# Output projections finished tile by tile over three slabs, and the first token tile turned inside the last slab

## The reference

```python
x = layer_norm(ALPHA * x + h, g, b)        # layers 0 and 1, three times each
x = x + gate * h;  n = rmsnorm(x)          # later layers (adaptive norm)
# h is always  (something of 256 x K) @ w_out, K = 1024, 2048 or 2816
# the next stage is always  norm(x) @ w_in
```

## Time and profile before

| | |
|---|---|
| time, median of 3 runs | 2055.17 us (2053.49 to 2056.4) |
| the profiled execution: its own time | 2055.43 us |
| the profiled execution: its span | 2053.7 us, so 1.73 us lie around it |
| PE busy | 1920.8 us, 94% of the span |
| POOL, DVE, ACT busy | 61%, 54%, 49% |
| mean granted TensorE clock | 0.977 of full speed |
| chain that ended last | PE 77%, DVE 11%, ACT 6%, POOL 3% |

### The profile page before, as it was taken

How to read it: one execution, slowest core, us unless ns; L and a number is a source line. 1 busy time by engine, 2 the same in 40 slices (tenths; PEclk the granted TensorE clock), 3 DMA queues, 4 the chain that set the end, 5 groups by cost and what they waited for, 6 DMA issues and landing times.

```text
span 2053.7 us, 34088 instructions
## 1 busy us (share of the span) xinstructions
PE 1920.8 (94%) x13629; PEld 1700.4 (83%) x13629; DVE 1109.8 (54%) x1524; ACT 998.6 (49%) x1726; POOL 1252.0 (61%) x585
## 2 busy tenths in 40 slices
PE   7989999999999989989999899898789999999997
PEld 7879799887999866868888788876579988968996
DVE  5472346623700172146667655678728962847981
ACT  4654345543444373435543444377845545525542
POOL 8768467686888405456778344300369886417995
PEclk9999999999999999999999899999999999999999
DMA  7435377774555405357764122211245554324552
GB/s 259 144 129 203 120 269 308 303 264 167 185 186 185 143 1 183 146 218 299 313 257 146 64 81 86 99 64 62 82 154 184 184 185 147 120 82 159 195 187 104
DMA packets 49217, 342.30 MB, mean 167 GB/s; under 512 B 5264, under 2 KB 7312, under 8 KB 8144
## 3 DMA queue, kind: packets, MB, share of 16 engines
q1 hardware_dynamic: 47440, 331.02, 44.1%
q0 software_dynamic: 1664, 9.70, 1.2%
HBM read 339.65 MB, written 1.05 MB: 166 GB/s over the span
## 4 chain that ended last, share of the span: by engine, by line
PE 77%; DVE 11%; ACT 6%; POOL 3%; issue 2%; DMA 1%; DVEq 0%; SPq 0%; ACTq 0%; POOLq 0%
PE bank L1708 13%; PE bank L1712 13%; PE bank L1763 13%; PE bank L1710 12%; PE bank L1813 3%; PE bank L1743 2%; PE bank L1742 2%; PE bank L1740 2%; PE bank L1939 2%; PE bank L1309 2%; PE bank L1311 2%; PE bank L1312 2%; ACT arena L1140 2%; DVE arena L723 2%; PE bank L1531 1%
## 5 line engine op out<-in xcount | busy, mean ns | idle before, releaser
L2219 POOL TENSOR_TENSOR w_lo<-ring,w_hi 128x1024 fp32r<-128x1024 f32 x360 | 877.0, 2465 | 275.2 <-ACT w_hi L2827 258.0
L1708 PE MATMUL bank<-x_hi,w_hi 128*128 128x256 f32 x2176 | 618.5, 284 | 18.6 <-POOL w_lo L2219 14.1
L1712 PE MATMUL bank<-x_lo,w_hi 128*128 128x256 f32 x2176 | 619.7, 285 | 0.0
L2827 ACT ACTIVATE w_hi<-ring 128x1024 fp32r<-128x1024 f32 x448 | 448.9, 1052 | 332.8 <-DMA ring<-slabs_dram 326.1
L1708 PEld LDWEIGHTS bank<-x_hi,w_hi 128*128 128x128 f32 x2176 | 415.8, 191 | 38.5 <-issue 37.3
L1712 PEld LDWEIGHTS bank<-x_lo,w_hi 128*128 128x128 f32 x2176 | 415.0, 191 | 0.0
L1710 PE MATMUL bank<-x_hi,w_lo 128*128 128x256 f32 x1472 | 414.3, 281 | 0.0
L1710 PEld LDWEIGHTS bank<-x_hi,w_lo 128*128 128x128 f32 x1472 | 282.4, 192 | 0.0
L2219 POOL TENSOR_TENSOR w_hi<-ring,w_hi 128x1024 fp32r<-128x1024 f32 x88 | 208.8, 2394 | 102.7 <-ACT w_hi L2827 102.7
L2751 ACT ACTIVATE arena<-bank 128x512 f32<-128x512 f32 (+1 forms) x178 | 97.9, 563 | 279.6 <-PE bank L1712 192.1
L1710 PE MATMUL bank<-x_hi,w_hi 128*128 128x256 f32 x704 | 197.5, 281 | 0.0
(11 more groups left out here) (355 smaller groups left out, 3665.1 us busy)
## 6 DMA issues: line engine op xcount, KB each, us to landing
ring<-slabs_dram SPq DMA_DIRECT2D x308, 1024.0 KB, 4.8
lnrow<-ln_dram POOLq DMA_DIRECT2D x6, 1024.0 KB, 5.3
arena<-slabs_dram SPq DMA_DIRECT2D x4, 1024.0 KB, 8.3
xt<-xT_dram SPq DMA_DIRECT2D x1, 1024.0 KB, 5.9
xt<-memT_dram SPq DMA_DIRECT2D x1, 1024.0 KB, 12.0
x<-x_dram SPq DMA_DIRECT2D x1, 1024.0 KB, 13.6
arena<-ctx_dram POOLq DMA_DIRECT2D x1, 1024.0 KB, 8.0
lnrow<-ln_dram POOLq DMA_DIRECT2D x2, 512.0 KB, 5.0
```

The lines of the kernel that those rows point to most:

```text
L1708: ins = pe.matmul(dst, wh[:, k, c], src[0][:, k, :], start=(k == 0), stop=False)
L1712: ins = pe.matmul(dst, wh[:, k, c], src[1][:, k, :], start=False, stop=(k == KC - 1))
L2219: pool.tensor_tensor(dst[:, c], ring[:, s, c], w_hi[:, s, c].bitcast(F32), ALU.subtract).then_inc(S["lo_ready"], 1)
L2827: a.activation(w_hi[:, g % RING, c], ring[:, g % RING, c], ACT.Copy) \
```

## The change

Five edits, which the diff below shows by their core.

1. `rows_split` takes `last` (3 unless given; `dwo` gives 2): the last three slabs, L-2, L-1 and L, run as tile 0 of all three, then tile 1 of all three. This holds for `xwo0`, `fo0`, `xwo1`, `fo1`, `ho0` and `ho1`. `swo`, `rows` (`gwo`, `pw2`) and `dwo` keep two.
2. `first_tile`: in `fo0`, `xwo1`, `swo`, `ho0` and `pw2` the transposes of tile 0 (with the gate rows in the later layers) are issued between the bank 2 and the bank 3 part of slab L, tile 1. `late_ada(.., 0)` and `(.., 1)` now both come before the transposes of tile 1.
3. DVE: in the norms after `fo0` and `xwo1` the two subtractions for tile 0 are put between the steps of tile 1's norm: one between the statistics of its two halves, one ahead of its centring. In `residual`, `row_var(0)` and `row_scale(0)` (or the final output of tile 0) come before `gate_times(2)`.
4. ACT: in the later layers `row_squares(2)` moves behind `tile_out` of bank 4, and `row_squares(3)` behind that of bank 5. In `x_to_T` both copies of the small products follow tile 0.
5. Input projections (`col_T_split`, `col_N_split`) run over chunks 0 to 3 for both halves of the bank and then over chunks 4 to 7, where each half of the bank took all eight chunks before; a slab's second low half is first needed after 24 matmuls and not after 12.

```diff
 # rows_split
-                last_two = (n_slabs - 2, n_slabs - 1)
-                for j in range(n_slabs - 2):
+                tail = range(n_slabs - last, n_slabs)
+                for j in range(n_slabs - last):
...
-                for j in last_two:
+                for j in tail:
                     ready_for(j)
-                    tile(j, 0, (0, 1), (0, 1), j == last_two[0])
-                tile(last_two[0], 1, (0, 1), (0, 1), False)
-                for h in range(2):
-                    tile(last_two[1], 1, (0, 1), (h,), h == 0)
+                    tile(j, 0, (0, 1), (0, 1), j == tail[0])
+                for j in tail[:-1]:
+                    tile(j, 1, (0, 1), (0, 1), j != tail[0])
+                tile(tail[-1], 1, (0, 1), (0,), True)
+                if first_tile:
+                    first_tile()
+                tile(tail[-1], 1, (0, 1), (1,), False)
 # tokens_to_T, rms_to_T: one tile each, called twice
+            def tokens_tile(tt, used_up=False, by_class=False, in_tail=0):
...
+                for q in range(2):
+                    b = 4 + 2 * tt + q
+                    pe.wait_ge(free_of(2 * tt + q), frees(2 * tt + q))
+                    pe.wait_ge(free_of(b), frees(b))
...
+                        ins = pe.transpose(dst, x[:, tt, c * P:(c + 1) * P], ident[:, :])
+                        begun(ins, used_up and c == 0)
+                    fill(ins, b, "act", "dve")
...
-            network(0)
+            network(0, lambda: tokens_tile(0, by_class=True, in_tail=1))
             late_ada(0, 0)
-            tokens_to_T(by_class=True, between=lambda: late_ada(0, 1))
+            late_ada(0, 1)
+            tokens_tile(1, by_class=True)
...
-            cross(1)
+            cross(1, lambda: tokens_tile(0, in_tail=1))
             late_ada(1, 0)
-            tokens_to_T(used_up=True, between=lambda: late_ada(1, 1))
+            late_ada(1, 1)
+            tokens_tile(1, used_up=True)
...
             for h in range(2):
+                if h:
+                    rms_tile(xn[0], (0, 5), 0)
                 swo_tile(7, 1, (0, 1), (h,), h == 0)
-            rms_to_T(xn[0], "h0", 0, 5)
+            rms_to_T(xn[0], "h0", (0, 5))
             network("h0")
-            rows_split("ho0")
+            rows_split("ho0", first_tile=lambda: rms_tile(xn[1], (1, 2), 0))
 # norm_stats (DVE); between(q) is split_tile(q, 0, ...) while tt == 1
                 for h in range(2):
                     b = 2 * tt + h
+                    if h and between:
+                        between(0)
...
+                if between:
+                    between(1)
                 centre(tt, 0, in_bank)
 # residual (DVE)
-                gate_times(2)
                 row_var(0)
-                added(2)
                 if stage:
                     row_scale(0, xn[n])
                 else:
                     to_out(0)
+                gate_times(2)
+                added(2)
 # rms_to_T (ACT)
-                for b in range(3):
+                for b in range(2):
                     row_squares(n, b)
                 a.wait_ge(S["mod_ready"], L.took("mod_ready"))
                 tile_out(layer, part, 0, 0)
+                row_squares(n, 2)
+                tile_out(layer, part, 0, 1)
                 row_squares(n, 3)
                 copy_out(0, gate_row[:, 0:512])
-                tile_out(layer, part, 0, 1)
 # col_T_split; col_N_split likewise
-                for ch in range(2):
-                    col_T_half(stage, u, ch, b, src, used_up, waits, last_net)
+                for at in (0, HC):
+                    for ch in range(2):
+                        col_T_half(stage, u, ch, b, src, used_up, waits, last_net,
+                                   range(at, at + HC), True)
```

More of the change, by code:

```diff
@@ L1266, in gate, with rms_tile, rms_to_T @@
                 fill(ins, b, "act")
-            def rms_to_T(src, stage, *row_of):
-                marks.setdefault("res", []).append(mark("dve"))
[L1271 to L1281, removed]
+            def rms_tile(src, row_of, tt):
+                gate(*row_of, tt)
+                for q in range(2):
+                    b = 4 + 2 * tt + q
+                    pe.wait_ge(S["n_ready"], L.took("n_ready"))
+                    pe.wait_ge(free_of(b), frees(b))
+                    for k in range(4):
+                        c = 4 * q + k
+                        ins = pe.transpose(bank[b][:, k * P:(k + 1) * P],
+                                           src[:, tt, c * P:(c + 1) * P], ident[:, :])
+                    fill(ins, b, "act")
+            def rms_to_T(src, stage, row_of):
+                marks.setdefault("res", []).append(mark("dve"))
+                rms_tile(src, row_of, 1)
                 marks.setdefault("gate", []).append(mark("act"))
@@ L1690, in pair, with col_T_half @@
                 return (FIRST[stage] + u) % RING
-            def col_T_half(stage, u, ch, b, src=(x_hi, x_lo), used_up=False, waits=None, last_net=False):
-                if ch == 0:
+            def col_T_half(stage, u, ch, b, src=(x_hi, x_lo), used_up=False, waits=None, last_net=False,
+                           chunks=range(KC), both=False):
+                if ch == 0 and 0 in chunks:
                     pe.wait_ge(free_of(b), frees(b))
@@ L1701, in col_T_half @@
                 dst, c = bank[b][:, ch * T:(ch + 1) * T], slice(ch * P, (ch + 1) * P)
-                for k in range(KC):
+                for k in chunks:
                     if ch == 0 and k % 4 == 0:
@@ L1736, in col_N_split, with rows_split @@
                 pe.wait_ge(free_of(b), frees(b))
[L1737 to L1744, removed]
+                for at in (0, HC):
+                    pe.wait_ge(S["lo_ready"], L.took("lo_ready"))
+                    for tt in range(NT):
+                        dst, t = bank[b][:, tt * 256:(tt + 1) * 256], slice(tt * P, (tt + 1) * P)
+                        for k in range(at, at + HC):
+                            ins = pe.matmul(dst, src[0][:, k, t], wh[:, k, :],
+                                            start=(tt == 0 and k == 0), stop=False, skip_group_check=True)
+                            begun(ins, tt == 0 and k == 0)
+                            pe.matmul(dst, src[0][:, k, t], wl[:, k, :], start=False, stop=False,
+                                      skip_group_check=True)
+                            ins = pe.matmul(dst, src[1][:, k, t], wh[:, k, :], start=False,
+                                            stop=(k == KC - 1), skip_group_check=True)
                 fill(ins, b, "act")
-            def rows_split(stage, src=(h_hi, h_lo), n_slabs=FC // 2, ready=("hT_ready", 2), hook=None):
+            def rows_split(stage, src=(h_hi, h_lo), n_slabs=FC // 2, ready=("hT_ready", 2), hook=None,
+                           last=3, first_tile=None):
                 second_first = stage in ("fo0", "fo1")
@@ L1834, in rows, with tokens_to_T @@
                 for h in range(2):
+                    if h and first_tile:
+                        first_tile()
                     tile(n - 1, 1, (0, 1), (h,), h == 0)
[L1837 to L1854 removed]
+            def tokens_tile(tt, used_up=False, by_class=False, in_tail=0):
+                if tt == 0:
+                    marks.setdefault("normed", []).append(L.now(("dve", 3)) + in_tail)
+                for q in range(2):
+                    b = 4 + 2 * tt + q
+                    pe.wait_ge(free_of(2 * tt + q), frees(2 * tt + q))
+                    pe.wait_ge(free_of(b), frees(b))
+                    for k in range(4):
+                        c = 4 * q + k
+                        dst = bank[b][:, k * P:(k + 1) * P]
+                        if by_class:
+                            dst = dst.rearrange("p (a b j) -> p j b a", a=4, b=4)
+                        ins = pe.transpose(dst, x[:, tt, c * P:(c + 1) * P], ident[:, :])
+                        begun(ins, used_up and c == 0)
+                    fill(ins, b, "act", "dve")
+            def tokens_to_T():
+                for tt in range(NT):
+                    tokens_tile(tt)
             def project(kind, stage, src):
@@ L2074, in _ @@
             rows_split("dwo", (x_hi, x_lo), 4, ("o_split", 2),
-                       lambda j: [turn_head(g) for g in (6, 7)] if j == 1 else None)
+                       lambda j: [turn_head(g) for g in (6, 7)] if j == 1 else None, last=2)
             while_norm("N", "xv0")
@@ L2341, in step, with norm_stats @@
                 v.wait_ge(S["v_step"], L.own("v_step"))
-            def norm_stats(tt, rows):
+            def norm_stats(tt, rows, between=None):
                 in_bank = rows < 5
```

87 lines of the change are left out of this document (46 added, 41 removed).

## The result

The changed kernel takes 2081.56 us (median of 4 runs, 2080.29 to 2083.2), the kernel before 2054.49 in the same session (4 runs, 2053.49 to 2056.4). The ratio is 1.0131, 95% interval 1.0114 to 1.0149: slower by 27 us, against a forecast of 2080.5 and a forecast loss of 25.1. The profiled execution after has a span of 2080.0 us, 26.3 more than before.

What follows compares the result with a forecast made beforehand. PE, busy 94% of the span, was taken as the bound, with idle time mostly at norms. Boundary and clock costs less gains of 1.6 and 0.9 summed to 25.1 us on 2055.43: 2080.5 us, range 2065 to 2090.

Steps and rivals of the forecast that it cites:

- The trigger decides: Six places with `last` = 3: next stage's slab 1 is issued 5.57 us later, tile 0 complete only 2.79 us earlier.
- Rival A: Late transfer hidden except after `xwo1` and `fo1`, where the chain shows it: 10.3 us lost, 2065.7 us; chance 0.12.
- B: Rival: norm bound by tile 0's completion, starting 2.79 us earlier at `fo0`, `xwo1`, `ho0`: 2044.5 us; chance 0.07.
- five signs: Issues 11.1 us apart; PE waits 8 us after `xwo1`, newly after `xwo0`; ACT releases `row_var(0)` after `ho0`; end 1.6 less.
- After `xwo1`: Chain moves 5.57 us and transposes delay bank 3: cost 5.4 to 6.6, taken 6.4, plus 0.5 for the clock.
- After `fo1`: Chain moves 5.57 us, `rstd` some 0.4 shorter: cost 5.1 to 5.6, taken 5.1, plus 1.2 for the clock.
- The collision: After `fo1`, DVE's two-input scaling could collide with POOL's delayed low parts; the sum would be 2081.0, not 2080.5.
- After `ho0`: Late slab 1 holds ACT ahead of the square sums, delaying transposes and bank 3: cost 5.8 to 7.1, taken 6.9.
- After `fo0`: Tile 0 normed 2.79 us earlier, but DVE waits for ACT's copies behind slab 1: cost 0.5 to 1.4, taken 0.9.
- After `xwo0`: Slab 1's high part moves 5.57 or 3.9 us, slack 1.2: cost 2.7 to 4.4, taken 3.6, plus 1.7 clock.
- Small ones: Costs of 0.9 after `swo` and 0.4 after `pw2`; gains of 0.9 at the start and 1.6 at the end.
- Sum: All costs less gains: 25.1 us lost, 2080.5 us; low bounds 17.2, high bounds 33.2.

Runs made afterwards that it cites:

- e_last2: Changed kernel with `last` = 2 in all of `rows_split`, everything else of the change kept: 2060.8 us, ratio 1.0027.
- e_only3: Kernel before with only the slab order of `last` = 3 (`dwo` keeps 2), no early transposes or reorderings: 2075.3 us, ratio 1.0101.
- e_free: Changed kernel with the next stage's slab 1 parts queued behind the norm on POOL and ACT, not ahead of it: 2051.25 us, ratio 0.9975.
- e_f3: e_bfree with `last` = 3 in all of `rows_split` except `dwo`, no early transposes: 2044.11 us, ratio 0.9957.
- e_best: e_f3 with slab 1's parts after `ho0` and `fo1` moved to where each boundary has room: 2043.12 us, ratio 0.9953.
- e_bfree: e_end plus the queue edits of e_free, slab order elsewhere as before, nothing turned early: 2055.25 us, ratio 1.0007.
- e_end: Kernel before with the input projections' new chunk order, `last` = 3 at `ho1` alone, and tile 0's final output early: 2051.78 us, ratio 0.9988.

## Why the prediction held, point by point

- **The trigger decides.** Shown from three sides: put back, 21 us return (e_last2); alone, it costs 20.6 (e_only3); with the norm out from behind it, the kernel is 3.5 us faster than before (e_free). The stages named for it, transfer, ACT, POOL, `rstd`, are the ones in the chain after. Rival A is out: the boundaries after `xwo0` and `ho0`, where the chain did not show the transfer, lost 4.7 and 9.1. B is out for this kernel. What it said of an early tile 0 came true in part in e_f3, when its condition was met by queue order and not by a faster slab: `fo0` and `xwo1` gain 2.0 and 1.7 of its 2.79, `ho0` nothing. That e_f3's 2044.1 us is close to B's 2044.5 is a coincidence: its other gains are not in B's sum. All five signs named beforehand came: issues 11.4 to 12.2 us apart, 8.34 us of waiting after `xwo1`, a new wait after `xwo0`, `row_var(0)` released by ACT, and 1.7 us less at the end.
- **After `xwo1`, 6.9 forecast, 7.6 measured.** Scaling moved by 9.51 - 3.60 (the shift already there at the start of `xwo1`) = 5.9. DVE began on bank 3 905.78 - 899.60 = 6.2 us later, where the working had 4.4 to 5.6: the last transposes took 1.12 and the six matmuls 2.57 at half clock.
- **After `fo1`, 6.3 forecast, 6.5 measured, by two misses that cancel.** The trigger cost 11.86 - 5.55 = 6.3, of which 0.5 is a new wait of PE for POOL at the last slab, and `rstd` gave 0.45 back (0.66 us, before 1.11). So the path took 5.9 where 5.1 was taken, and about 0.6 is left for the lower clock where 1.2 was taken. The collision that I weighed by the Trainium skill (SBUF — State Buffer, "SBUF: two separate sides") did not come: the low part ended at 1137.0, before the scaling at 1137.76, which took 0.76. So the rule had nothing to act on here. The row of e_best above agrees with it: a step with `x` and `lnrow` as inputs took 2.85 us beside POOL's low part. In e_free a scaling with one tensor input (TENSOR_SCALAR at 1125.87) was slowed as well, 2.77 us beside the low part begun at 1125.74, where the one at 1123.57 took 0.75; the two-input rule that I quoted does not cover that one.
- **After `ho0`, 6.9 forecast, 9.1 measured.** The term furthest outside its own bounds (5.8 to 7.1). PE's 0.84 us wait for the last slab's low part at 1728.60 was missing from the working; it delays slab 1's issue by as much. Transposes at half clock (1.97 us, taken as 1.3) stand ahead of bank 3's matmuls, and again in the second half (0.4). Order alone costs 4.5 and the rest of the change alone 1.3: together they cost 3.3 more than the sum. The rows fit this: PE stands 4.94 us in front of the transposes while the norm is late, with bank 3's matmuls behind, and 0.16 us in e_last2.
- **After `fo0`, 0.9 forecast, 1.0 measured, for half the reason.** DVE does wait 2.00 us for ACT behind slab 1, and moving that slab gives 2.0 back (e_free). But the working missed that `last` = 3 alone gains 1.9 here and that the early transposes cost 2.0 even with an early slab (e_last2). Two misses that cancel.
- **After `xwo0`, 5.3 forecast with its clock, 4.7 measured.** The new waits of 1.40 and 0.92 us and the clock of 0.74 are there; e_only3 gives the same 4.6. The two waits make 2.3 us, below the bounds of 2.7 to 4.4, and the remaining 2.4 go with the lower clock, where 1.7 was taken: again two misses that cancel in part. (The working also gives the new gap as 1.5 to 3.3 us beside a cost of 2.7 to 4.4, as if the slack of 1.2 were taken off twice.)
- **Small ones.** `swo` 0.2 for 0.9, outside its 0.5 to 1.5, and start -1.1 for -0.9. The end gave -1.4 for -1.6: from PE's last matmul (2070.08) to DVE's last output at 2074.00 it is 3.92 us, before 2047.74 - 2042.16 = 5.58. `pw2` is 1.3 for 0.4, outside its 0 to 1, but e_bfree shows 1.3 with this boundary as in the kernel before, so it need not be the edit's.
- **Sum.** 27.9 against 25.1, mostly `ho0`; the stages' own -1.6 bring the span to 26.3. The mechanism held; that the time came within 1.1 us is partly luck. The forecast was put on the profiled execution's 2055.43 us, 0.9 above the median of the kernel before in the session that measured the change, and by medians the loss is 27.1, 2.0 more than forecast.
- **Open.** Why the stages between the boundaries differ by up to 7 us between profiles; what decides whether the first context CAST ahead of `fo1`'s norm takes 2 us or 9; whether early transposes could pay at any boundary with its own queue order, and what they cost without the reorderings. No kernel here isolates these.

## What to carry to other kernels

When an order of work is changed to finish one tile early, ask first which release of a buffer moves with it, and then what stands behind the refilled buffer's conversions in the queues of the other engines. Instructions for the next stage belong behind the norm's own steps wherever the next stage can spare them, and ahead of them where cover work needs them: the same move gained 30 us in one kernel and lost a boundary in another. Before work is put in front of the last matmuls of a bank, check that its input is ready by then, since PE carries the whole delay into that bank.

## What the runs showed of the hardware

- After waits of the same length the clock can be different. After `pw2`, e_end and e_bfree have the same order and the same wait, and PE's timeline of e_end shows:

```profile
1848.31 1.18 PE L1282 MATMUL bank<-ident,arena 128*128 128x128 f32 x8 [3.44 <-DVE arena L520]
```

  The eight transposes behind a wait of 3.44 us take 1.18 us there (granted clock 0.76 in 1848.3 to 1850.3) and 1.97 in e_bfree (0.50 in 1852.7 to 1854.7), and the next stage starts 1.3 us later. The kernel before and e_f3 show 1.18, e_only3 and e_best 1.97. Each kernel here has one profile, so it stays open whether this changes from one execution to the next or is fixed by what ran earlier. A difference of 1.3 us at a gap of this length proves nothing about an edit.
- A DVE instruction can stand until POOL pauses. In the changed kernel the CAST at 1099.92 took 9.24 us while POOL worked on low parts without a pause; it ended at 1109.16, inside POOL's first idle time (1108.88 to 1109.27). In e_free it was 9.19 us, ending at 1093.40 in a pause from 1093.12 to 1093.60. The same CAST took about 2.0 us in the six other kernels of the experiments, and 4.3 in the kernel before, where it got through without a pause of POOL.
- The mean granted clock goes roughly with the time of a run: the eight runs of e_last2 lie between 2055.2 us (0.976) and 2063.18 (0.970), without an edit between them. A single profile shows which wait decides at a boundary, and its size to about 1.3 us; it is not good for the total.
